# Sorting the tokens of a grouped mixture of experts into two full tiles: 16 expert visits in place of 20

## The reference, cut to what matters

```python
def _hier_moe(x, wg, bg, we, be, w_gate, w_up, w_down):
    glog = (jnp.einsum('bsd,dg->bsg', x, wg) + bg).astype(F32)
    gp, gi = lax.top_k(jax.nn.softmax(glog, -1), 1)
    elog = (jnp.einsum('bsd,gde->bsge', x, we) + be).astype(F32)
    elog = jnp.einsum('bsge,bsg->bse', elog, jax.nn.one_hot(gi[..., 0], N_GROUPS, dtype=F32))
    ep, ei = lax.top_k(jax.nn.softmax(elog, -1), TOP_K)
    ep = ep / jnp.sum(ep, -1, keepdims=True)
    eid = gi * EXPERTS_PER_GROUP + ei
    combine = jnp.sum(jax.nn.one_hot(eid, N_EXPERTS, dtype=F32) * (gp * ep)[..., None], axis=2)
    h = jax.nn.silu(jnp.einsum('bsd,edf->bsef', x, w_gate)) * jnp.einsum('bsd,edf->bsef', x, w_up)
    h = h * combine[..., None].astype(h.dtype)
    return jnp.einsum('bsef,efd->bsd', h, w_down)
```

## Time and profile before

| what | us |
|---|---|
| median of three runs | 1607.17 (1603.54 to 1612.1) |
| the profiled execution | 1611.87 |
| its span, first to last instruction | 1610.0 |
| mean granted PE clock | 0.925 of 2.4 GHz |
| busy: PE / DVE / ACT / POOL | 1402.5 / 926.3 / 781.2 / 660.7 |
| experts of one layer, first up matmul to last down matmul | 205.7, twice |
| DMA over the whole run | 305 MB, 190 GB/s |

### The profile page before, as it was taken

How to read it: one execution, slowest core, us unless ns; L and a number is a source line. 1 busy time by engine, 2 the same in 40 slices (tenths; PEclk the granted TensorE clock), 3 DMA queues, 4 the chain that set the end, 5 groups by cost and what they waited for, 6 DMA issues and landing times.

```text
span 1610.0 us, 19353 instructions
## 1 busy us (share of the span) xinstructions
PE 1402.5 (87%) x6260; PEld 1115.9 (69%) x6260; DVE 926.3 (58%) x1400; ACT 781.2 (49%) x1171; POOL 660.7 (41%) x557
## 2 busy tenths in 40 slices
PE   6979789999967899988889789888798796998886
PEld 2757577888856688867767577666577675876664
DVE  8684944122364411136575567888665664678886
ACT  4323354444543344434454356666445443566662
POOL 2877797977765599965002500000140025000000
PEclk8989999999987899999988789999899787899998
DMA  9665557644343355535220238888452203388881
GB/s 386 263 233 209 213 205 278 225 157 145 143 144 143 106 192 194 183 134 205 96 93 1 105 117 316 314 315 313 181 209 105 79 1 105 130 325 315 317 315 75
DMA packets 47660, 305.24 MB, mean 190 GB/s; under 512 B 5805, under 2 KB 9133, under 8 KB 12110
## 3 DMA queue, kind: packets, MB, share of 16 engines
q1 hardware_dynamic: 40594, 288.99, 47.8%
q10 hardware_dynamic: 6974, 15.08, 2.6%
HBM read 299.86 MB, written 4.19 MB: 189 GB/s over the span
## 4 chain that ended last, share of the span: by engine, by line
issue 36%; POOL 33%; PE 23%; DVE 4%; ACT 1%; DVEq 1%; POOLq 0%; ACTq 0%
POOL w_lo L571 32%; PE G L1035 4%; PE G L1037 4%; PE G L1036 4%; PE AC L1035 3%; PE AC L1037 3%; PE AC L1036 3%; DVE w_lo L1698 1%; PE AC L1604 1%; POOL arena L590 1%; DVE arena L2457 1%; PE T L1627 1%; ACT arena L998 1%; ACT w_hi L606 1%; PE T L1074 0%
## 5 line engine op out<-in xcount | busy, mean ns | idle before, releaser
L571 POOL TENSOR_TENSOR w_lo<-w_raw,w_hi 128x512 fp32r<-128x512 f32 (+1 forms) x520 | 636.3, 1259 | 494.3 <-ACT w_hi L606 493.9
L606 ACT ACTIVATE w_hi<-w_raw 128x1024 fp32r<-128x1024 f32 x496 | 509.3, 1058 | 370.8 <-PE AC L1037 173.9
L1698 DVE TENSOR_TENSOR w_lo<-w_raw,w_hi 128x1024 fp32r<-128x1024 f32 x270 | 316.9, 1220 | 27.3 <-ACT w_hi L606 25.6
L1035 PE MATMUL G<-w_hi,xT_hi 128*128 128x512 f32 x432 | 183.1, 424 | 29.9 <-POOL w_lo L571 20.0
L1035 PE MATMUL AC<-w_hi,yT_hi 128*128 128x512 f32 x480 | 194.6, 405 | 13.8 <-DVE w_lo L1698 4.4
L1037 PE MATMUL AC<-w_hi,yT_lo 128*128 128x512 f32 x480 | 190.8, 398 | 0.0
L1036 PE MATMUL AC<-w_lo,yT_hi 128*128 128x512 f32 x480 | 190.8, 398 | 0.0
L1036 PE MATMUL G<-w_lo,xT_hi 128*128 128x512 f32 x432 | 175.6, 406 | 0.0
L1037 PE MATMUL G<-w_hi,xT_lo 128*128 128x512 f32 x432 | 175.1, 405 | 0.0
L1035 PE MATMUL G<-w_hi,arena_r 128*128 128x512 f32 x320 | 133.4, 417 | 0.0
L1037 PE MATMUL G<-w_hi,arena_r 128*128 128x512 f32 x320 | 126.7, 396 | 0.0
(11 more groups left out here) (413 smaller groups left out, 1961.4 us busy)
## 6 DMA issues: line engine op xcount, KB each, us to landing
w_raw<-w_stream SPq DMA_DIRECT2D x152, 1024.0 KB, 4.8
w_raw<-w_expert SPq DMA_DIRECT2D x120, 1024.0 KB, 4.9
mod<-rows ACTq DMA_DIRECT2D x2, 2048.0 KB, 10.6
rel_scratch<-arena ACTq DMA_DIRECT2D x1, 3072.0 KB, 18.2
mod<-rows ACTq DMA_DIRECT2D x3, 476.0 KB, 3.1
x_sb<-x SPq DMA_DIRECT2D x1, 1024.0 KB, 9.4
arena<-const SPq DMA_DIRECT2D x1, 1024.0 KB, 9.6
mod<-gn_g ACTq DMA_DIRECT2D x1, 1024.0 KB, 6.9
```

The lines of the kernel that those rows point to most:

```text
L571: i = pool.tensor_tensor(w_lo[:, k % SLOTS, cols], w_raw[:, k % RAW, cols], w_hi[:, k % SLOTS, cols].bitcast(F32), ALU.subtract)
L606: act.activation(w_hi[:, k % SLOTS, :], w_raw[:, k % RAW, :], ACT.Copy).then_inc(hi_ready, 1)
L1035: pe.matmul(out, xh, wh, start=start, stop=False)
L1698: dve.tensor_tensor(w_lo[:, k % SLOTS, :], w_raw[:, k % RAW, :], w_hi[:, k % SLOTS, :].bitcast(F32), ALU.subtract).then_inc(lo_ready, 1)
```

## The change

Tokens are sorted into exactly two tiles of 128, without empty slots. The groups are ranked by size, and the places are ordered so that the largest group lies second: it alone can reach over the border of the two tiles (`TILES_OF`). There are 16 visits; of each four, the first (the largest group, `ORDER`) works on both tiles, the other three on one. The expert weights of every visit are now fetched by a row number that DVE computes, so SP waits for `og_ready` and loads four registers before the layer's first expert piece. ACT no longer casts expert units ahead during the output product (`end=L_MOE`); it casts the first four between the copies of the gather, and POOL splits them then.

Further: the Silu waits for its own up units only; the two G banks take turns; PE does one up unit of v + 1, then the transposes of v, then the rest; the router of token tile 0 runs ahead of the transposes of tile 1; the token copy `xk_hi` goes behind the casts of the turned tiles. In the first block the rotation reads PSUM directly (no copy), POOL waits for `att_ready` before it splits the four units of the attention's output product, and the angles move into the first two feed-forward iterations, with their sines ahead of the last one's step on ACT.

The diff, cut to its core:

```diff
-VISITS = EXPERTS + EPG
-GTILES = EGROUPS + 1
-SLOTS_X = GTILES * P
+VISITS = EXPERTS
+ORDER = (1, 0, 2, 3)
+TILES_OF = ((0,), (0, 1), (1,), (1,))
+LAST_VISIT = (VISITS - 3, VISITS - 1)
...
+                sp.wait_ge(og_ready, l + 1)
+                row = [sp.value_load(og_i[0:1, o:o + 1], min_val=0, max_val=(EGROUPS - 1) * EPG * E_PIECES) for o in range(EGROUPS)]
...
+                        sp.wait_ge(lo_ready, n + (L_MOE + PIECE * (p + 1) - RAW))
+                        expert_piece(row[ORDER[u % EPG]] + (l * (EXPERTS * E_PIECES) + u // EPG * E_PIECES + j), p % n_ring)
...
+            for k in range(U_ATT_OUT // RAW * RAW, U_WO):
+                if k == U_ATT_OUT:
+                    pool.wait_ge(att_ready, 1)
+                lo(0, k, UNIT // 2)
...
+                if e == FF_TILES - 1:
+                    act.wait_ge(ang_ready, 1)
+                    act.activation(sinM, sm[:, 64:96].rearrange("p (t n) -> p t n", t=TOK), ACT.Sin)
+                    act.activation(cosM, sm[:, 96:128].rearrange("p (t n) -> p t n", t=TOK), ACT.Sin).then_inc(trig_ready, 1)
...
-                down_his(n, L_OUT, t + LT_OUT, 4, gate_and_roots)
+                down_his(n, L_OUT, t + LT_OUT, 4, gate_and_roots, L_MOE)
...
+                gathered(0)
+                gathered(1)
+                his(L_MOE, L_MOE + 1, n)
+                gathered(2)
+                his(L_MOE + 1, L_MOE + 2, n)
+                gathered(3)
+                his(L_MOE + 2, L_MOE + UP, n)
...
+                    act.wait_ge(unit_used, n + done(L_MOE + UP + 6 * v - (2 if v else 0)))
...
+                    if t == 0:
+                        pe.wait_ge(x2_ready, l * TOK + 2)
+                        turn_x(tb + (LT_X2 + 2), 1, x_sb)
...
+                        for i_t, b in zip(visit_tiles(v), visit_banks(v)):
+                            if u == 0 and v and b in visit_banks(v - 1):
+                                pe.wait_ge(ffn_h, l * VISITS + (FF_TILES + v))
...
                 for v in range(VISITS):
+                    if v + 1 < VISITS:
+                        visit_up(v + 1, range(1))
                     visit_turn(v)
                     if v + 1 < VISITS:
-                        visit_up(v + 1)
+                        visit_up(v + 1, range(1, UP))
                     visit_down(v)
...
+                dve.tensor_tensor(t1, p1, s, ALU.mult)
+                dve.tensor_tensor(t2, p2, s, ALU.mult)
+                dve.tensor_tensor(x1, p1, c, ALU.mult)
+                dve.tensor_tensor(x2, p2, c, ALU.mult).then_inc(g_free, 1)
...
+            for e in range(2):
+                lo(e * 2 + T_MLP, yT_hi, yT_lo, 0, 4)
+                mlp_hidden(e + 1)
+                if e == 0:
...
+                    angles(0.0, sm[:, 64:96])
+                    dep()
+                else:
+                    angles(0.25, sm[:, 96:128]).then_inc(ang_ready, 1)
...
+                dve.scalar_tensor_tensor(g_key, count, 4.0, tie, ALU.mult, ALU.add)
+                dep()
+                dve.tensor_tensor(bigger, by_h(g_key), by_g(g_key), ALU.is_gt)
+                dep()
+                dve.tensor_reduce(g_pos, bigger, AX.X, ALU.add)
...
+                dve.tensor_copy(og_i[:, :], g_row).then_inc(og_ready, 1)
...
+                for t in range(TOK):
+                    dve.tensor_scalar(hot[:, t, :], slot_iota, s_slot[:, t, :], None, ALU.is_equal).then_inc(route_in, 1)
```

More of the change, by code:

```diff
@@ L117 @@
 LT_MOE = LT_X2 + 4
-LT_VISIT = LT_MOE + 2 * KC
+LT_VISIT = LT_MOE + UP
 LT = LT_VISIT + VISITS
@@ L619, in turn_hi, with down_his @@
                                    T[:, t, 0:nch * P].rearrange("p (c n) -> p c n", n=P), ACT.Copy).then_inc(t_hi, 1)
-            def down_his(n, k, t, pairs, after=None):
+            def down_his(n, k, t, pairs, after=None, end=None):
                 for q in range(pairs + 1):
@@ L1655, in _ @@
+                        i.then_inc(unit_used, 1)
+                visit_up(0, range(UP - 1))
+                pe.wait_ge(route_in, l * 4 + 4)
+                for i_t in range(2):
                     for t in range(TOK):
-                        i = pe.matmul(G[:, 1, g * EPG:(g + 1) * EPG], hot[:, t, g * P:(g + 1) * P].bitcast(F32), r_1[:, t, :], start=t == 0, stop=t == 1)
+                        i = pe.matmul(T[:, 0, i_t * 16:(i_t + 1) * 16], hot[:, t, i_t * P:(i_t + 1) * P].bitcast(F32),
+                                      comb[:, t, :, :].rearrange("p o e -> p (o e)"), start=t == 0, stop=t == 1)
@@ L1662, in _ @@
                     visit_down(v)
-                    if v == 0:
-                        turn_hot(0, EGROUPS)
-                    if v == 2:
-                        turn_hot(EGROUPS, GTILES)
-                def scatter(t, g0, g1):
-                    for g in range(g0, g1):
-                        for b in range(2):
-                            for y in (xg_hi, xg_lo):
-                                i = pe.matmul(AC[:, 2 * t + b, :], hotT[:, g, t * P:(t + 1) * P], y[:, 4 * b:4 * b + 4, g * P:(g + 1) * P],
-                                              start=g == 0 and y is xg_hi, stop=g == GTILES - 1 and y is xg_lo)
-                    return i
@@ L1677, in _, with scatter @@
-                pe.wait_ge(my_lo, l * GTILES * 2 + 2 * EGROUPS)
-                scatter(0, 0, EGROUPS)
-                pe.wait_ge(my_lo, l * GTILES * 2 + 2 * GTILES)
-                scatter(0, EGROUPS, GTILES).then_inc(acc_ready, 1)
-                scatter(1, 0, GTILES).then_inc(acc_ready, 1)
+                def scatter(t, i_t):
+                    for b in range(2):
+                        for y in (xg_hi, xg_lo):
+                            i = pe.matmul(AC[:, 2 * t + b, :], hotT[:, i_t, t * P:(t + 1) * P], y[:, 4 * b:4 * b + 4, i_t * P:(i_t + 1) * P],
+                                          start=i_t == 0 and y is xg_hi, stop=i_t == 1 and y is xg_lo)
+                    return i
@@ L1683, in _ @@
+                pe.wait_ge(my_lo, l * 4 + 2)
+                scatter(0, 0)
+                pe.wait_ge(my_lo, l * 4 + 4)
+                scatter(0, 1).then_inc(acc_ready, 1)
+                scatter(1, 0)
+                scatter(1, 1).then_inc(acc_ready, 1)
         @block.vector
@@ new lines, in _ @@
+                dep()
+                dve.tensor_tensor(g_place, g_pos, g_swap, ALU.add)
+                dep()
+                dve.tensor_tensor(below, by_h(g_place), by_g(g_place), ALU.is_lt)
+                dve.tensor_tensor(placed, by_h(g_place), by_g(place), ALU.is_equal)
+                dep()
+                dve.tensor_tensor(below, below, by_h(count), ALU.mult)
+                dve.tensor_tensor(placed, placed, by_h(g_first), ALU.mult)
+                dep()
+                dve.tensor_reduce(g_start, below, AX.X, ALU.add)
```

337 lines of the change are left out of this document (162 added, 175 removed).

## The result

The changed kernel took 1527.4 us (median of four runs, 1523.3 to 1530.9), the kernel before 1609.6 beside it (four runs, 1603.5 to 1613.1). The ratio is 0.949, 95% interval 0.945 to 0.953: 5.1% faster. The profiled execution of the changed kernel took 1528.1 us, with a span of 1526.2 and a mean granted clock of 0.928.

The account below looks back on a forecast made before the run. Expert stage bound by PE's work plus one hand-off per visit, first block by PE with stalls. Two layers' 70.4 us plus 14 from the first block, 84.4, off 1611.9 gave 1527.5, or 1523 against the median; range 1500 to 1562.

Parts of the forecast that it names:

- PE gets nothing back from the sorting itself: Expert visits: 20 tile-visits and 720 matmuls before and after; only weight work falls, 96 units in place of 120.
- the hand-off: Each expert visit: down matmuls, then Silu, product and PE's transposes in turn; costs PE 1.4 us per visit.
- 18 matmuls, 4.1 us: Between up phase and transposes, two down units and one up unit cover a chain of 2.0 to 2.5 us.
- the weight ring: Single visits: slot free to unit split takes 2.7 us against 4.1 for three units, so PE isn't starved.
- rival (a): Expert visits: the hand-off stays, 1.4 us in each of 15 visits, 21 per layer: 1565 us; chance 0.08.
- POOL paces up(0): Start of expert stage: POOL needs 2.77 us per unit; fourth unit ready at 19.6, up(0) ends at 22.4.
- Rival (e): Start of expert stage: longer idle puts more PE matmuls at half clock, 5 us per layer: 1533 us; chance 0.08.
- the merges: First block: sixteen merges take 3.4 us unhindered instead of 12.6 beside POOL; gain 8 us, between 5 and 10.
- POOL's units follow at PE's pace: First block, after POOL's wait for att_ready: only four units queue behind it; part of the 8 us gain.
- (b): Single expert visits: DMA capped at 320 GB/s, 9.8 us against 8.4, some 12 us per layer: 1547 us; chance 0.11.
- (d): Expert weight pieces can't overlap, 4.9 us each; 36 us lost per layer: 1665 us, slower; chance 0.02.
- (c): First block: its edits give nothing because POOL or PE paces it anyway: 1537 us; chance 0.09.

Follow-up runs that it names:

- both edits undone: The kernel after, but each Silu waits for the previous visit's down matmuls again and PE transposes ahead of all the next visit's up matmuls: 1572.7 us.
- The late Silu alone: The kernel after, but each Silu waits for the down matmuls of the visit before again, PE's order kept: 1566.7 us, ratio to before 0.976.
- the kernel where DVE splits: The kernel after, but DVE instead of POOL splits the first four expert units, between its splits of the gathered tokens: 1521.7 us.

## Why the prediction was right, and where it was off

The forecast was 1523, and 1527.5 for an execution like the profiled one; measured were 1527.4 and 1528.1.

**The visits.** Right in the mechanism: "PE gets nothing back from the sorting itself" is what the table shows. With the hand-off gone before and after have stages of the same length; with it left in, the sorting gives 7.7 us per layer. The stage lost 31.2 us, and the hand-off's edits alone, on the old tiles, took away 31.3. The pace of 8.4 us per single visit came as worked out, and from up(1)'s first matmul to the end of the last down it took 158.8 us where the terms gave 159.6. Not in the 1.4 us per visit was the clock: with the hand-off, before ran 6.8 us per layer at half, in visit 1 and in the last visit, and this went too.

Off was the account of why it fits. "18 matmuls, 4.1 us" took the down units and the one up unit as one cover. The down units alone, 2.7 us, are enough; the up unit alone is not, and more than half of what that costs comes from ACT's and DVE's weight splits, which queue behind the waiting Silu; the rest is the double visits' wait for their banks. The prediction named what is late next (the weight ring), but not that a late wait on ACT delays it. The rival (a), the hand-off stays, had its price nearly right: it gave 21 us per layer, and with both edits undone the stage is 23.6 longer. The late Silu alone costs 21 too, but by the queue and the banks, not by PE's wait for the product ahead of its transposes.

**The start.** The terms, counted from the gather's start: first unit raw at 7.4, measured 6.2 (the row numbers were written 2.6 us after the ranks, for 2.7, and the four register loads with the first issue took another 2.6, for 3.6); first up matmul at 11.4, measured 10.3; next up unit at 25.6, measured 27.1. The step that failed is "POOL paces up(0)". PE paced it, at half clock: its first unit took 5.3 us for 2.7, a loss of 2.5 us in place of the 1.0 taken. Two smaller things: the 12 small products between up(0)'s third and fourth unit take 1.2 us, for which the sum had no term, and the wait for the product behind up(0) is 1.6 us for the 2.2 taken. Rival (e) was thus half true, and that the sum of the start still came within 1.5 us is in part luck: it began 1.1 us sooner than predicted. From the gather to the last down it was 185.9 us for 185.2.

**Router and scatter.** The stretch from the last wait ahead of the router to the gather is 1.9 us shorter in either layer, for 2.0. From the last down matmul to the residual it takes 3.4 us:

```profile
1101.63 1.07 PE L1684 MATMUL AC<-arena_r,xT_hi 128*128 128x512 f32 x4
...
1103.80 3.02 PE L1684 MATMUL AC<-arena_r,xT_hi 128*128 128x512 f32 x12 [1.11 <-DVE arena_r L2509]
...
1105.03 1.22 DVE L2092 SCALAR_TENSOR_TENSOR x_sb<-x_sb,AC 128x1024 f32<-128x1024 f32 x1 [1.29 <-PE AC L1684]
```

Before it was 4.7, so 1.3 us are gained for 1.4.

**The first block.** Sum 14 taken; 12.6 by position (eight profiles with the edits against three without), 10.0 by the medians, 13.7 by the ratios. Rotation: 3.9 for 3. Its four products with PSUM take 0.68 us each where they took 1.27 to 1.78, and POOL runs on. The gain did not come from the stall of 7.6 us that the prediction pointed at, which is still 7.1 us long; it came from the many small waits for POOL ahead of matmuls on AC, 7.2 us in all before (50 to 240 us) and 3.5 after (50 to 235). Angles: PE's wait for the first square fell from 7.1 to 2.2 us and the sines cost 1.7 (PE waits 3.8 instead of 2.1 us at the last step), 3.2 net for 2.9; by position it is 3.1. The mis-sized term is the merges: 5.6 for 8. PE did come 8.1 us sooner to its first transposes, but had lost 2.7 of it by those of the merged heads, at 471.64. It lost 1.6 in the wait of 2.17 us shown above, where it was 0.60. Before, ACT had an activation and a cast (L774, L613) done while PE waited for the merges; now they stand between PE's first transposes and their split:

```profile
450.73 1.02 ACT L774 ACTIVATE arena<-AC 128x1024 f32<-128x1024 f32 x1 [1.60 <-PE AC L1051]
...
451.65 1.05 ACT L613 ACTIVATE w_hi<-w_raw 128x1024 fp32r<-128x1024 f32 x1
452.60 0.65 ACT L625 ACTIVATE yT_hi<-T 128x256 fp32r<-128x256 f32 x2
```

It lost another 1.5 in a stall of 4.5 us for 3.0, for which the list of waits names no releaser; the transposes start 0.1 us after DVE's third addition of the merged heads has ended. The first two additions have both inputs in SBUF. POOL's postponed splits now run beside them, and they take 2.85 us (the first row, of after). In the kernel without POOL's wait POOL is idle there, and they take 1.29 (the second row, of that kernel):

```profile
465.80 2.85 DVE L1996 TENSOR_TENSOR arena<-arena 128x512 f32<-128x512 f32 x2
...
471.15 1.29 DVE L1990 TENSOR_TENSOR arena<-arena 128x512 f32<-128x512 f32 x2
```

The step that was too simple is "POOL's units follow at PE's pace": the wait moved part of the contention, and didn't end it. Some 0.4 us came back, since the first transposes themselves took less.

The terms as measured sum to 81.4 us: 62.4 for the two stages, 6.4 for router and scatter, 12.6 for the first block. The two profiled executions are 83.8 us apart, where 84.4 was forecast. The stage and the first block each fell a little short, and 2.4 us between the two traces belong to no term.

**The rivals not yet named.** (b) and (d), a DMA limit or pieces that can't overlap, fell with 369 GB/s held for 120 us. (c), the first block gives nothing, fell with the kernel that undoes it.

## What to carry to other kernels

When an engine hands over to a second and third and waits for the result, look at what the waiting instruction counts: a wait one phase too late cost more here through the work queued behind it on that engine's program than through the hand-off itself (12.6 us of 21 went when one unit's cast and split moved ahead of it). Count the bottleneck engine's own work before and after a reordering of data; if it is the same, ask which of the edits that come with it takes the idle time away, and whether that edit could be made without the rest. And at the start of a stage that depends on fresh data, two things end last in turn: the first weights' way through their splits, and PE's clock after the idle stretch. An operation that is moved so that it no longer delays one neighbour should be priced beside its new neighbours too.

## What the runs showed of the hardware

- PE's granted clock. In the kernel where DVE splits it stood at 0.50 (1.2 GHz) from 894 to 925 us, through the router's small matmuls and most of the gather, and in after PE's first up matmuls ran at that level until 931.7. With three filler matmuls ahead of the ranks and eight ahead of the gather the clock was full (2.4 GHz) 1.1 us ahead of the gather or 1.1 us into it, which then took 4.1 or 4.6 us for 6.6. Two idle stretches of 1.6 and 1.5 us lost it again in one layer; 1.1 and 1.5 us in the other layer of the same run did not, and neither did 1.1 and 0.4.
- DMA. 369 GB/s were held over 120 us with 0.97 of the DMA engines busy, where before and after show about 300: their 300 was what the kernels asked for, not a limit.
- DVE beside POOL. In after, with POOL splitting, most of DVE's operations on 2 to 32 columns behind the Exp took 0.54 to 0.65 us; with the same splits on DVE and POOL idle they took 0.14 to 0.19, so that moving 4.9 us of splits onto DVE delayed it less than its sum. The merges of two SBUF tiles started 0.27 us apart for 1.28 in the same way, and the two additions above took 1.29 us for 2.85.
